# A two-block network on one core: per-crossing waits in place of the all-engine barriers between its 25 sections

## The reference: what is computed

```
x = first_block(x, mem, ...)         # norm, 5 branches, gates, output projection, norm, residual
x = second_block(x, mem_2, ...)      # even layer, odd layer, final norm

# first block, branches on h = rms_norm(x), each 512 wide, with its own gate silu(z):
#  A gated delta rule (4 heads, a scan over 8 chunks of 128 tokens)   B 31-tap convolution + layer norm
#  C sliding-window attention with sinks   D linear recurrence        E attention on a 256-token memory
merged = sum_n sigmoid(gates_n) * (y_n @ w_br[n]);   x = x + rms_norm(merged @ w_out)

# even layer: dilated attention (4 heads x 3 groups), pooling at 4 scales, memory attention
x = x + (concat(a, b, m) * silu(z)) @ w_out
# odd layer: spatial gating in chunks of 128, memory attention
x = x + (concat(c, m) * silu(z)) @ w_out
```

## Time and profile before

| | us |
|---|---|
| median of 3 runs | 4184.78 (4181.14 to 4186.34) |
| the profiled execution's own span, first to last instruction | 4184.3 |
| PE busy with matmuls | 3564.8 (85%) |
| DVE busy | 2057.3 (49%) |
| POOL busy | 1343.4 (32%) |
| ACT busy | 919.5 (22%) |

### The profile page before, as it was taken

The page is one execution under the profiler, slowest core; times in us unless marked ns, Lnnn a source line. Parts: engine busy times, 40 slices in busy tenths (PEclk is TensorE's granted clock), DMA queues, the critical chain, the costliest instruction groups (busy, mean ns, idle before and its releaser), DMA issues.

```text
span 4184.3 us, 42906 instructions
## 1 busy us (share of the span) xinstructions
PE 3564.8 (85%) x16732; PEld 2843.2 (68%) x16732; DVE 2057.3 (49%) x2359; ACT 919.5 (22%) x1681; POOL 1343.4 (32%) x595
## 2 busy tenths in 40 slices
PE   5898999998978999879798786969659988989987
PEld 3676898876755667657576475757547766677765
DVE  3666232327995555754631547465443543213444
ACT  2323112222002342323102221222211112200121
POOL 1332442224642224433343122212105423224533
PEclk8999999999989999989899898989879999999999
DMA  3121122112222012121121110001011101111211
GB/s 128 41 63 53 56 66 61 56 51 71 56 76 65 23 28 61 33 78 33 55 90 41 63 31 25 26 21 31 21 33 61 46 21 41 51 49 32 71 30 55
DMA packets 301341, 208.44 MB, mean 50 GB/s; under 512 B 25797, under 2 KB 277577, under 8 KB 301033
## 3 DMA queue, kind: packets, MB, share of 16 engines
q1 hardware_dynamic: 270192, 131.62, 11.4%
q10 hardware_dynamic: 30969, 74.26, 4.8%
HBM read 172.01 MB, written 33.83 MB: 49 GB/s over the span
## 4 chain that ended last, share of the span: by engine, by line
PE 65%; DVE 22%; ACT 4%; issue 3%; ACTq 1%; PEld 1%; DMA 1%; DVEq 1%; POOL 1%; PEldq 0%; POOLq 0%
PE ps L347 48%; PE ps L1236 4%; DVE wrk L648 3%; PE ps L778 3%; DVE wrk L627 2%; PE ps L521 1%; ACT wrk L806 1%; PE ps L791 1%; PE ps L1585 1%; PE ps L1835 1%; DVEq L2209 1%; DVE wrk L856 1%; DVE h_lo L559 1%; DVE wrk L529 1%; DVE wrk L831 1%
## 5 line engine op out<-in xcount | busy, mean ns | idle before, releaser
L2260 POOL TENSOR_TENSOR w_hi<-w_raw,pool_one 128x1024 fp32r<-128x1024 f32 x295 | 579.7, 1965 | 2765.1 <-PE ps L347 2757.7
L347 PE MATMUL ps<-h_hi,w_hi 128*128 128x512 f32 x2928 | 1213.0, 414 | 249.5 <-DVEq L2220 145.4
L347 PE MATMUL ps<-h_hi,w_lo 128*128 128x512 f32 x2928 | 1161.7, 397 | 0.0
L347 PE MATMUL ps<-h_lo,w_hi 128*128 128x512 f32 x2928 | 1161.4, 397 | 0.0
L347 PEld LDWEIGHTS ps<-h_hi,w_hi 128*128 128x128 f32 x2928 | 563.3, 192 | 425.4 <-issue 237.4
L2262 POOL TENSOR_TENSOR w_lo<-w_raw,w_hi 128x1024 fp32r<-128x1024 f32 x295 | 763.7, 2589 | 23.2
L347 PEld LDWEIGHTS ps<-h_hi,w_lo 128*128 128x128 f32 x2928 | 561.7, 192 | 122.6
L347 PEld LDWEIGHTS ps<-h_lo,w_hi 128*128 128x128 f32 x2928 | 564.5, 193 | 114.3 <-issue 8.7
L347 PE MATMUL ps<-y_hi,w_hi 128*128 128x512 f32 (+1 forms) x896 | 347.3, 388 | 54.6 <-DVEq L2209 24.1
L347 PE MATMUL ps<-y_lo,w_hi 128*128 128x512 f32 (+1 forms) x896 | 332.7, 371 | 0.0
L347 PE MATMUL ps<-y_hi,w_lo 128*128 128x512 f32 (+1 forms) x896 | 332.5, 371 | 0.0
(11 more groups left out here) (318 smaller groups left out, 4005.5 us busy)
## 6 DMA issues: line engine op xcount, KB each, us to landing
w_raw<-in_w_in SPq DMA_DIRECT2D x87, 512.0 KB
w_raw<-in_even_w_in SPq DMA_DIRECT2D x48, 512.0 KB
away<-wrk ACTq DMA_DIRECT2D x80, 256.0 KB, 2.0
wrk<-away ACTq DMA_DIRECT2D x32, 512.0 KB
w_raw<-in_odd_w_in SPq DMA_DIRECT2D x32, 512.0 KB
x_fm<-acc ACTq DMA_DIRECT2D x2, 4096.0 KB, 12.2
w_raw<-in_w_br SPq DMA_DIRECT2D x32, 256.0 KB
w_raw<-in_even_w_out SPq DMA_DIRECT2D x24, 256.0 KB
```

The costliest lines, as they stand in the source:

```text
L347: mm = nc.tensor.matmul(ps[:, b, 0:n], l, r, start=(k == 0 and q == 0), stop=(k == nk - 1 and q == 2))
L2260: nc.gpsimd.tensor_tensor(w_hi[:, s], w_raw[:, s], one, ALU.mult).then_inc(hi_ready, 1)
```

## The change

The barrier in `play` is gone: 25 drains and 50 waits on each of three engines. Each engine's instructions stand in the same order as before, on all five engines; only what they wait for differs. In its place stand, where data crosses from one thread to another:

- PE's first tile of section 1 (`A beta alpha`) waits k-block by k-block for the normed x (`x_parted`), and so does the load of the first memory.
- `gate_z` of branch B waits for branch B's normed tiles (`ln_finished`).
- `x back` (the load of x for the residual) waits for the last gating of branch E, and the post norm for that load (`x_is_back`). A stage of its own closes the post norm on DVE (`post_added`), for which the spill of x waits.
- In the heads, the value transposes and `z_act` wait for the head's rotation (`rope_done`); ACT's take-outs into a head's tiles wait for the join of two heads before (`head_free`, `join_done`), those of `pool x` for join 2 and of `even q` for join 3.
- The pooling sums wait for `pool x`, `even out A` for join 3 (PE) and for the restored x (DVE), the odd layer norm for its projection, the load of `odd q k v` for the first odd gating.

The core of the diff:

```
-    at_end = {e: sig.sem(f"{e}_at_section_end") for e in engines}
...
-    def add_out(name, r):
+    def add_out(name, r, y_there=None, sum_there=None):
         def f_pe(pe):
-            return dense_run(pe, r, rhs_y, rhs_y)
+            if y_there:
+                y_there(pe)
+            yield from dense_run(pe, r, rhs_y, rhs_y)
         def f_dve(dve):
+            if sum_there:
+                sum_there(dve)
...
+    project("A beta alpha", r_ba, lambda j, b: wt(10, b), lambda j: col("b_ba", 0),
+            ready=lambda pe, k, b: pe.wait_ge(x_parted.sem, x_parted.nth(b * KD + k)))
...
         def m_load(act, mem=mem):
+            act.wait_ge(x_parted.sem, x_parted.nth(2 * KD - 1))
...
+    def tiles_gated(act):
+        act.wait_ge(e_done.sem, e_done.nth(7))
...
     def x_back(act):
+        tiles_gated(act)
         load(act, wrk[:, 0:8, :], x_fm.rearrange("k p t -> p k t"))
         yield 0.9
         loads_done(act)
+        act.drain().then_inc(x_is_back.sem, 1)
...
+    def post_done(dve):
+        dve.drain().then_inc(post_added.sem, 1)
+    stage("post norm added", 0.1, dve=post_done)
...
+    def head_free(act, h):
+        if h >= 2:
+            act.wait_ge(join_done.sem, join_done.nth(h - 2))
...
         project("head v", r_v, lambda j, b: head_tile(h, 6)[:, b * HALF:(b + 1) * HALF],
-                ready=ready)
+                before=lambda act, j, b: head_free(act, h), ready=ready)
...
         def vt_pe(pe):
+            pe.wait_ge(rope_done.sem, rope_done.nth(h))
...
-    project("even q", run(2, *both(w2, C2_Q)), to_tiles(4))
+    project("even q", run(2, *both(w2, C2_Q)), to_tiles(4), before=lambda act, j, b: head_free(act, 5))
...
-    add_out("even out A", run(4, *both(w2o[0], 0), 4, 4))
+    add_out("even out A", run(4, *both(w2o[0], 0), 4, 4),
+            lambda pe: pe.wait_ge(join_done.sem, join_done.nth(3)),
+            lambda dve: dve.wait_ge(x_is_back.sem, x_is_back.nth(1)))
...
     def play(name, eng):
         chains[name] = Chain(eng, f"{name}_chain")
-        for n, plan in enumerate(plans):
+        for plan in plans:
             threads = [thread_part(name, eng, t, row) for t, row in plan.items()]
             due = [next(th, None) for th in threads]
             while any(d is not None for d in due):
                 i = min((d, i) for i, d in enumerate(due) if d is not None)[1]
                 due[i] = next(threads[i], None)
-            eng.drain().then_inc(at_end[name], 1)
-            for other in engines:
-                if other != name:
-                    eng.wait_ge(at_end[other], n + 1)
```

More of the change, by code:

```diff
@@ L652, in conv, with layer_norm @@
         ch.after(max(last))
-    def layer_norm(name, tile, nk, width, g, tmp, finish=None, us=50.0):
+    def layer_norm(name, tile, nk, width, g, tmp, finish=None, us=50.0, ready=None):
         sq, rs = tmp
@@ L663, in layer_norm @@
         scaled = sig.take("ln_scaled", 2 * nk)
+        finished = sig.take("ln_finished", 2 * nk)
         at = lambda first, share, b, k: first + share * (b * nk + k) / (2 * nk)
@@ L930, in _hybrid @@
     stage("store x", act=store_x)
-    norm_acc("norm x", "g_pre")
+    x_parted = norm_acc("norm x", "g_pre")
     w_in = weights("w_in")
@@ L1371, in _hybrid @@
     stage("B conv", 145.0, dve=b_conv)
[L1372 removed]
+    b_normed = layer_norm("B norm", lambda k, b: wt(4 + k, b), 4, W, lambda k: col("b_ln_g", k), (8, 9),
                lambda k, b: nc.scalar.activation(wt(4 + k, b), wt(4 + k, b), ACT.Silu, bias=col("b_ln_b", k)))
@@ L1385, in _hybrid @@
     on("dense")
-    gate_z("B z", run(2, *both(w_in, C_BZ)), lambda j, b: wt(4 + j, b), lambda j: col("b_bz", j), 10)
+    gate_z("B z", run(2, *both(w_in, C_BZ)), lambda j, b: wt(4 + j, b), lambda j: col("b_bz", j), 10,
+           o_ready=lambda j, b: (b_normed.sem, b_normed.nth(4 * b + j)))
     b_gated = sig.take("b_gated", 1)
@@ L1688, in _hybrid @@
     on("aux")
+    x_is_back = sig.take("x_is_back", 2)
     def x_back(act):
+        tiles_gated(act)
         load(act, wrk[:, 0:8, :], x_fm.rearrange("k p t -> p k t"))
@@ L1702, in _hybrid @@
     norm("post norm", acc_at, HALF, post, sq=8, rs=9)
+    post_added = sig.take("post_added", 1)
+    def post_done(dve):
+        dve.drain().then_inc(post_added.sem, 1)
+    stage("post norm added", 0.1, dve=post_done)
     section()
@@ L1729, in by_residue @@
         return ap.rearrange("p (i r) -> p r i", r=16)
+    rope_done = sig.take("rope_done", 4)
+    join_done = sig.take("join_done", 4)
+    def head_free(act, h):
+        if h >= 2:
+            act.wait_ge(join_done.sem, join_done.nth(h - 2))
     def project_head(h, pace=1.0, ready=None):
@@ L1924, in d_dve @@
             nc.vector.tensor_tensor(y_lo[:, h, :], out_t[0], y_hi[:, h, :].bitcast(F32), ALU.subtract)
+            dve.drain().then_inc(join_done.sem, 1)
         stage("maxima spread", 6.0, pe=lambda pe: spread(pe, st_m))
@@ L1951, in _hybrid @@
         else:
-            project("pool x", run(2, *both(w2, C2_X)), acc_at)
+            r_px = run(2, *both(w2, C2_X))
+            project("pool x", r_px, acc_at, before=lambda act, j, b: head_free(act, 4))
         on("aux")
@@ L1974, in p_dve @@
             yield i / 4
+            for b in range(2):
+                out_taken(dve, r_px.t0 + i, b)
             x, src, s = acc[:, i, :], acc[:, i, :], 1
@@ L2036, in _hybrid @@
     w3o = A["odd_w_out_2"][0].rearrange("(b k p) n -> b p k n", b=3, p=P)
-    project("odd v", run(4, *both(w3, C3_V)), to_tiles(0), ready=part_ready(h_parted))
+    r_ov = run(4, *both(w3, C3_V))
+    project("odd v", r_ov, to_tiles(0), ready=part_ready(h_parted))
     section()
@@ L2043, in _hybrid @@
     layer_norm("odd ln", lambda k, b: wt(k, b), KD, D, lambda k: col("odd_ln_g_2", k), (8, 9),
-               lambda k, b: nc.scalar.activation(wt(k, b), wt(k, b), ACT.Identity, bias=col("odd_ln_b_2", k)))
+               lambda k, b: nc.scalar.activation(wt(k, b), wt(k, b), ACT.Identity, bias=col("odd_ln_b_2", k)),
+               ready=lambda pe, b: out_taken(pe, r_ov.t0 + 7, b))
     section()
@@ L2125, in _hybrid @@
     on("dense")
-    gate_z("odd z", run(2, *both(w3, C3_Z)), wt, None, 10)
+    odd_first = gate_z("odd z", run(2, *both(w3, C3_Z)), wt, None, 10)
     add_out("odd out", run(4, *both(w3o[0], 0), 4, 4))
@@ L2137, in _hybrid @@
     on("aux")
-    fetch("odd q k v", [(j, at_oq + j) for j in range(4)] + [(8, at_kv[2]), (9, at_kv[2] + 1)], 44.0)
+    fetch("odd q k v", [(j, at_oq + j) for j in range(4)] + [(8, at_kv[2]), (9, at_kv[2] + 1)], 44.0,
+          lambda act: act.wait_ge(odd_first.sem, odd_first.nth(7)))
     def odd_wait(dve):
```

13 lines of the change are left out of this document (11 added, 2 removed).

## The result

The changed kernel takes 4154.31 us (median of 4 runs, 4152.38 to 4155.0), the kernel before in the same comparison 4185.56 (4181.14 to 4188.6): ratio 0.9924, 95% interval 0.991 to 0.9938. The predicted time was 4159. The profiled execution spans 4152.2 us where the one before spans 4184.3: 32.1 us less, and 25.7 were forecast.

The account below looks back on a forecast made before the run. PE was taken as the bound, busy 3564.8 of 4184.3 us, with about 234 us under barriers as ceiling. Terms 3.7 + 3.0 + 4.5 + 0.8 + 2.8 + 5.7 + 4.7 + 0.5 = 25.7 us gave 4159 us, range 4146 to 4173.

Parts of the forecast that it names:

- The two questions: At each boundary: how much PE has ahead of its next wait, and what that wait is for.
- The rival of a full give-back: All barrier idle time returns, 234 us, to 3951, if PE could pass over a waiting instruction; chance 0.01.
- Section 1: First tile starts as k-blocks arrive; second transposes L1160 at 92.3 in place of 95.95: 3.7 us, between 0 and 6.1.
- A lead, once won, is kept: Whole kernel: everything behind a lead hangs on PE or on transfers that PE's progress releases, so the 25.7 us stay.
- Section 4: PE loses its 2.87 us stop and the 1.6 us restart, with 192 matmuls free: 4.5 us in full.
- slower rival: POOL splits slow DVE's tails; 13 hit casts at 2.07 us cancel the gain, 24 give 4209; nothing or slower 0.03.
- Heads: Sections 10 to 13: six matmuls run warm inside the stop, 0.7 us each, 2.8 us together (0 to 5.6).
- that rule's bound: Heads: if transposes don't count as PE activity like matmuls, the four heads give 0, the sum 2.8 us less.
- Sections 14 and 15: PE runs one free tile in the join; last take-out at x's landing, 6.7 us sooner: 5.7 us (3 to 8.5).
- The 1.0 us that I took off: Section 14: deducted from 6.7 us because POOL's split may slow a DVE cast in the join's tail.
- Sections 17, 19, 21 to 23: PE waited only for DVE's last operation, four stops of 0.97 us and one of 0.80: 3.9 + 0.8 us.
- The rest: Sections 2, 6 to 9, 16, 18, 20, 24 need what ended last; only the barrier's hop goes: 0.5 us.

Follow-up runs that it names:

- the kernel with the 20.8 us stage: Changed kernel with an empty 20.8 us stage ahead of each head's aux work, putting two tiles (96 matmuls) ahead of the value transposes: 4168.36 us, ratio 0.9959.

## Why the prediction was right, point by point

**The two questions were the right ones.** How much PE has ahead of its next wait, and what that wait is for, told where the 234 us would go: most of them stand in the changed trace as other waits. The rival of a full give-back failed for the reason given. That PE works its queue from the front was then shown by experiment: with 48 more matmuls ahead, the same kernel gains another 46.6 us.

**Section 1.** Forecast 3.7 at the second transposes, measured 4.7 (91.25 against 95.95 in the earlier trace rows), with the restart at 8.54 us close to the 8.27 taken; the first transposes ran at 82.71 where I had 84.0, so the load came 1.3 us sooner than I took it. The step that failed is the sentence "A lead, once won, is kept": section 2, for which I had no loss at all, took 3 us of it back, by two stops for DVE each with a spell at the half clock behind it.

**Section 3.** Forecast 3.0, measured 3.2. The load landed inside the bracket, and the half clock of 0.50 fell behind it, as written.

**Section 4.** Forecast 4.5 in full, measured 6.6. The stop and restart were sized right; 1.7 of the other 2.1 is the POOL split that no longer meets DVE's convolution, a gain by the same mechanism that my slower rival was built on. The last 0.4 is not followed.

**Section 5.** Forecast 0.8, measured 0.7.

**Heads.** The six matmuls run inside the stop and 28.48 us of it are left, as written. Forecast 2.8, measured 4.6, 4.0 and, with only these barriers back, about 6. The half clock did not last longer for the transposes. Stretches of the kernel before, from its restart in section 11 with six matmuls ahead of the transposes:

```profile
2615.70:2619.70 4.00, 3.92 (x14) 3.02 (x14) 0.00 (x0) 0.00 (x0) 0.00 (x0) 0.61 0.00 0
2619.70:2623.70 4.00, 3.98 (x18) 3.31 (x19) 0.00 (x0) 1.03 (x1) 0.00 (x0) 1.00 0.02 4
```

4 us x 0.39 = 1.6 us lost there, 4 x 0.45 = 1.8 in the changed kernel from 2601 on, and the clock is 1.00 in the second 4 us of both. The Trainium skill (TensorE: Matmul & The Clock Gate, Part 4: PE-mode transpose) has the transposes not count as PE activity in the way matmuls do; the trace shows no longer spell for it here. I took the middle between that rule's bound and the other, and the upper half was nearer.

**Sections 14 and 15.** Forecast 5.7, measured 7.2, within its bounds. The small pooling load took 2.85 us from its issue to the next one, which waits for it (3112.65, 3115.50), where I estimated 3. The 1.0 us that I took off is there: the join's tail on DVE, 25.15 us before (3102.65 to 3127.80), lasts 26.11 now, most of the difference in one group of three operations. Timeline of DVE, that group in the kernel before and in the changed one:

```profile
3117.28 3.50 DVE L1915 TENSOR_TENSOR wrk<-wrk 128x1024 f32<-128x1024 f32 x3
```

```profile
3101.13 4.26 DVE L1950 TENSOR_TENSOR wrk<-wrk 128x1024 f32<-128x1024 f32 x3
```

What ended the lead was another wait. The second load of x is issued 23.7 us after the start of the pooling sums (3116.16 to 3139.87), 27.35 before (3131.46 to 3158.81). I had the sums as fixed ("which don't move"). Two POOL splits fell into them before and one falls into them now, and each holds two of their small operations. Timeline of DVE in the kernel before, one held and one not:

```profile
3141.43 0.17 DVE L1978 COPY wrk<-wrk 128x4 f32<-128x4 f32 x1
...
3145.80 2.25 DVE L1983 TENSOR_TENSOR wrk<-small,acc 128x16 f32<-128x16 f32 x1
```

One split fewer makes the sums 3.6 us shorter. So the load doesn't bind, and the last take-out comes when PE's six remaining groups of 24 matmuls are done, 38.99 us behind the join's end in place of 46.94. That makes the term 1.3 to 1.5 us larger. My sum had this step wrong: the last take-out did not come at the landing of x, the sign that I had named, but behind PE.

**Sections 17, 19, 21 to 23.** Forecast 4.7, measured 5.7 on a trace that had section 17 at its slower length, and 2.5 against the kernel with barriers back. The stops of 0.97 are not gone: PE still stands 0.26 us at each (3353.67, for one), so that 0.7 of the 0.97 that I took in full is won, and a little of the rest goes back behind. The second figure is the fairer one: the term was too large by some 2 us.

**The rest.** 0.5 forecast, some 3.6 measured outside section 2, the largest 1.7 us in section 20 and 1.9 in section 9. Section 7 lasts 1.6 us longer (103.9 for 102.3) in most kernels without barriers and not in all. In sections 7 and 20 it is the clock. Section 7 in the kernel before, then in the changed one:

```profile
2172.50:2274.80 102.30, 92.71 (x386) 73.18 (x384) 18.85 (x18) 8.97 (x15) 34.60 (x16) 0.93 0.27 88
```

```profile
2161.20:2265.10 103.90, 95.67 (x386) 75.07 (x384) 19.06 (x18) 8.97 (x15) 34.60 (x16) 0.90 0.24 78
```

The same matmuls take 3 us more of PE at a granted clock of 0.90 for 0.93, and a part of that comes out of idle time. In section 20 the clock is 0.95 where it was 0.93. Why the clock differs there is open, and section 9 I have not followed.

**The sum.** Measured against the execution profiled before, 32.1 us; some 6 of them are that execution's own sections 1 and 17, and against the kernel with barriers back, whose profiled span is 4178.4, the gain is 26.2; but that execution was 3.5 us faster than its kernel's median, and by the medians of these two kernels it is 29.4. Against the kernel before, the medians say 31.3, with an interval from 26 to 38. So the forecast of 25.7 is at the low end of what was measured, and its parts missed in both directions, by -3.5 us in section 2 and by some 2 to 3 in section 4 and in the rest. That these errors nearly cancelled is luck; the mechanism holds, the single terms hold to 2 or 3 us at best.

The slower rival's mechanism is real, 0.96 us in the last join, but its hits stayed far from the 13 that it needed, and the hits that went away outweigh it: 1.7 us in section 4, and 3.6 us of DVE's time in the pooling sums, of which at most the 1.3 to 1.5 above reached PE. What cost more, 3 us in section 2, was no rival of mine.

## What to carry to other kernels

A barrier between stages is worth what the engines behind it can do before their own next wait, and not the idle time booked on it: 234 us stood there and about 30 came out. Once it is gone, the instruction order decides, so change it next: an empty 10.4 us stage that put one tile ahead of the waiting transposes brought 46.6 us more here, and nothing while the barriers stood; but work moved into a stop is taken from a later place, and the second tile cost more than it gave. A lead of a few us also shifts which operations of PE, DVE and POOL meet; such shifts cost 3 us in one section, most of it by the clock, and gave 2 in another, so terms below some 3 us should be held with bounds on both sides.

## What the hardware showed unexpectedly

The clock can fall to half at a place in one execution and stay full at the same place in another. Section 16 ends in both programs with the same rows on PE: a stop of 2.05 us, 8 transposes, a stop of 1.11 us, 4 matmuls, then the barrier's stop of 0.97 us (0.98). Stretches from those 4 matmuls into section 17, in the kernel before:

```profile
3374.00:3379.00 5.00, 3.78 (x4) 1.19 (x5) 0.69 (x1) 0.20 (x1) 0.00 (x0) 0.50 0.00 0
3379.00:3383.00 4.00, 3.98 (x10) 3.13 (x11) 0.00 (x0) 0.00 (x0) 0.00 (x0) 0.50 0.01 4
```

The same with all barriers back:

```profile
3371.00:3376.00 5.00, 2.97 (x12) 1.42 (x12) 0.69 (x1) 1.02 (x1) 0.00 (x0) 1.00 0.00 0
3376.00:3380.00 4.00, 3.94 (x17) 3.30 (x18) 0.00 (x0) 0.00 (x0) 0.00 (x0) 1.00 0.00 0
```

Behind the barrier, ten matmuls against seventeen in 4 us. But the half clock was there already ahead of the barrier: the 4 matmuls took 3.78 us before and 1.98 with all barriers back. So the stop of 0.97 us did not bring it. The changed kernel with the barrier ahead of section 1 back bears this out: PE stands only 0.26 us at the start of section 17, the same 4 matmuls take 3.78 us, and the section lasts 98.1 us. The 2.9 us by which section 17 differs between the two profiles are this spell: 2.0 us in the 4 us shown, the rest beside them. What makes the clock fall in one execution and not in the other is not shown.

Three of DVE's SCALAR_TENSOR_TENSOR operations took 3.92 us alone and 5.63 beside a split on POOL. A cast of 128x1024 in the join, 0.69 us alone (3110.46 in the changed kernel), took 2.71 beside a split in the kernel with the 20.8 us stage:

```profile
2608.95 2.71 DVE L1958 CAST y_hi<-acc 128x1024 fp32r<-128x1024 f32 x1
```
